# Norms at the start and between the blocks: root, squares and scaled tiles in PSUM, and the mean asked for elsewhere

## Chip, cores and metric

One core of a Trainium2 chip runs the kernel. The metric is the device time of one execution in microseconds (us), as the median of several runs. Before: 1818.57 us, median of 3 (1818.01 to 1822.48).

## What is computed

A transformer block pair on 512 tokens of width 1024, all in fp32. Block one: h = x + mixer(rms_norm(x)), then a gated ffn; block two the same with memory attention beside two others. Of this only the four norms named here and the small projections next to them matter:

```python
def rms_norm(x, g):
    y = x * rsqrt(mean(x * x, axis=-1) + eps)
    return y * g

u = rms_norm(x, norm_mix_g); z = u @ w_in                 # n_mix, the kernel's first work
h = h + (silu(g) * up) @ w_down                           # down1a, down1b: end of block one
x2 = rms_norm(h, norm_final_g)                            # n_fin
mkv = rms_norm(mem, g_mem) @ w_mem_kv                     # n_mem; mk and mv, 256 memory rows
u2 = rms_norm(x2, g_mix_pre_2); z2 = u2 @ w_in_2          # n_mix2
bias = rel_bias[rel_bucket(...)]                          # from buckets and relb, by two small matmuls
```

## The kernel before, in words

Activations lie transposed: 8 tiles (KT) of 128 rows by 512 tokens. A product in fp32 quality is made of three matmuls of the fp32r type, high by high, high by low and low by high (`split_mm`, lines 378 to 380); each side is split into a rounded high part and the rest.

The weights are one stream of 278 units of 128x1024. SyncE loads a unit into `w_raw` (three slots, R = 3), ScalarE copies it rounded into `w_hi` (`feed`, line 820), GpSimd subtracts to get `w_lo` (`low_part`, line 335), TensorE uses it. `feed_after(t)` makes unit t+2 and waits until unit t-1 has been used up. ScalarE, VectorE and GpSimd each work through one queue in program order, so a feed stands behind what was issued before it.

`tile_unit` is 24 matmuls into one bank, `token_unit` 12, `two_units` runs two units at once, tile k as soon as the norm's low part k is there. `down` runs eleven units over the ffn's hidden tiles into four banks. `acquire(b)` waits until the bank's last result was copied out.

A norm goes like this. ScalarE squares tile k (`square`), VectorE adds it to tmp[2] (`add_square`, line 1343), TensorE multiplies the sum by a matrix of ones to get the sum over rows (`norm`, line 514, bank 2), ScalarE makes the root with Ln and Exp into tmp[3] (`root`, lines 849 and 851). `norm_split` then runs on VectorE: scaled tile = hT x gain x root (line 1361), ScalarE copies it rounded to `u_hi` (line 864), VectorE subtracts to get `u_lo` (line 1355). Scaled tiles rotate through four buffers. For n_fin the product goes back into hT (line 1688) and the squares for n_mix2 follow it tile by tile.

The places: n_mix is the first thing the kernel does, its mean ahead of the first two units (gif and qkb 0), with the two bias matmuls behind these (lines 600, 601). n_mem's mean is asked for after down1a's first unit. n_fin's is asked for between mk 1 and mk 2, n_mix2's between mv 2 and mv 3; mk units use banks 4 and 5 in turn, mv units banks 6 and 7. ScalarE copies mk 0 and 1 out behind n_fin's root, mk 2 and 3 behind squares 3 and 5 of n_mix2, and feeds four units behind squares 0, 2, 4 and 6. In front of n_mix2's root it has the feeds behind mv 2 and mv 3's places in the stream, the last of which waits for the end of mv 2.

## Time and profile before

| what | us |
|---|---|
| median of 3 runs | 1818.57 |
| the profiled execution | 1820.88, its span 1819.1 |
| TensorE matmul busy | 1726.2, 95% of the span |
| VectorE busy | 869.7, 48% |
| GpSimd busy | 704.9, 39% |
| ScalarE busy | 625.1, 34% |

The span runs from the first instruction to the last. Busy time of TensorE is modelled at the ends of matmuls, so an idle stretch looks up to 0.2 us shorter than the time between two matmuls of a stream. In brackets behind a row stands the idle time before it and what ended it. The granted clock is the share of TensorE's full clock that the chip allows.

### The profile page before, as it was taken

The numbers are of one execution on the slowest core, as the hardware profiler recorded it, in microseconds if no ns is written. First come the engines' busy times: TensorE is split into PE (matmuls) and PEld (weight loads), VectorE is DVE, ScalarE is ACT, GpSimd is POOL, SyncE is SP. The second block draws the span as 40 slices with busy tenths as digits, with TensorE's granted clock in tenths as the row PEclk, the third lists the DMA queues.
The fourth block names the chain that finished last, engine by engine and source line by source line (L and its number), as shares of the span: only waits on it lengthen the run. The fifth ranks groups of instructions, "written<-read, shape, count | busy, mean of one in ns | idle before, by whom it ended". The sixth has DMA issues, their size and how long they took to land.

```text
span 1819.1 us, 23230 instructions
## 1 busy us (share of the span) xinstructions
PE 1726.2 (95%) x7880; PEld 1356.0 (75%) x7888; DVE 869.7 (48%) x1341; ACT 625.1 (34%) x997; POOL 704.9 (39%) x293
## 2 busy tenths in 40 slices
PE   5999999999999999998899899999999699999995
PEld 4888666777888887886578655668888488888884
DVE  6603665573655552035497756541332755555003
ACT  5233444434222223234424444453222422222221
POOL 2544222244544444444243111224444444444442
PEclk9999999999999999999999999999999899999998
DMA  4434311223322232234122111112332132232321
GB/s 154 160 130 117 103 58 47 69 72 115 113 94 92 94 103 93 93 104 151 61 93 74 43 36 35 59 45 95 94 102 93 36 115 92 92 103 94 103 93 46
DMA packets 46189, 162.21 MB, mean 89 GB/s; under 512 B 5564, under 2 KB 5692, under 8 KB 45864
## 3 DMA queue, kind: packets, MB, share of 16 engines
q1 hardware_dynamic: 42576, 151.16, 25.4%
q10 hardware_dynamic: 3544, 10.13, 1.7%
q8 instruction: 43, 0.70, 0.2%
q14 instruction: 26, 0.21, 0.0%
HBM read 156.91 MB, written 4.76 MB: 89 GB/s over the span
## 4 chain that ended last, share of the span: by engine, by line
PE 53%; issue 29%; POOL 10%; DVE 6%; ACT 2%; POOLq 0%; DVEq 0%; ACTq 0%
PE ps L378 16%; PE ps L380 16%; PE ps L379 16%; POOL w_lo L335 10%; PE ps L537 1%; PE ps L558 1%; DVE tmp L1343 1%; DVE tmp L1793 1%; PE ps L574 1%; PE ps L749 1%; DVE sum L1763 1%; PE ps L705 1%; DVE hT L1798 1%; PE ps L771 0%; PE ps L514 0%
## 5 line engine op out<-in xcount | busy, mean ns | idle before, releaser
L335 POOL TENSOR_TENSOR w_lo<-w_raw,w_hi 128x1024 fp32r<-128x1024 f32 x278 | 686.7, 2472 | 1068.4 <-ACT w_hi L820 1068.3
L378 PE MATMUL ps<-u_hi,w_hi 128*128 128x512 f32 x1392 | 565.1, 406 | 37.5 <-DVE u_lo L1355 11.6
L380 PE MATMUL ps<-u_hi,w_lo 128*128 128x512 f32 x1392 | 546.3, 392 | 0.0
L379 PE MATMUL ps<-u_lo,w_hi 128*128 128x512 f32 x1392 | 545.8, 392 | 0.0
L820 ACT ACTIVATE w_hi<-w_raw 128x1024 fp32r<-128x1024 f32 x278 | 292.7, 1055 | 425.5 <-PE ps L380 384.9
L378 PEld LDWEIGHTS ps<-u_hi,w_hi 128*128 128x128 f32 x1392 | 263.1, 189 | 117.0 <-issue 54.2
L380 PEld LDWEIGHTS ps<-u_hi,w_lo 128*128 128x128 f32 x1392 | 263.2, 189 | 56.4
L379 PEld LDWEIGHTS ps<-u_lo,w_hi 128*128 128x128 f32 x1392 | 263.6, 189 | 52.9 <-issue 2.4
L378 PE MATMUL ps<-a_hi,w_hi 128*128 (+1 forms) x352 | 137.2, 390 | 0.3 <-POOL w_lo L335 0.3
L380 PE MATMUL ps<-a_hi,w_lo 128*128 (+1 forms) x352 | 137.0, 389 | 0.0
L379 PE MATMUL ps<-a_lo,w_hi 128*128 (+1 forms) x352 | 137.0, 389 | 0.0
L1655 DVE TENSOR_TENSOR a_lo<-tmp,a_hi 128x512 f32 (+1 forms) x44 | 115.8, 2632 | 5.2
L1160 ACT ACTIVATE tmp<-tmp 128x512 f32<-128x512 f32 x44 | 27.8, 632 | 222.0 <-DVEq L1645 221.9
L1651 DVE TENSOR_TENSOR tmp<-ps,tmp 128x512 f32<-128x512 f32 x44 | 30.4, 692 | 100.5 <-PE ps L380 100.2
L378 PEld LDWEIGHTS ps<-a_hi,w_hi 128*128 128x128 f32 x352 | 66.1, 188 | 14.4 <-issue 0.8
L379 PEld LDWEIGHTS ps<-a_lo,w_hi 128*128 128x128 f32 x352 | 66.1, 188 | 13.8
L380 PEld LDWEIGHTS ps<-a_hi,w_lo 128*128 128x128 f32 x352 | 66.1, 188 | 13.7
L1643 DVE TENSOR_TENSOR tmp<-ps,tmp 128x512 f32<-128x512 f32 x44 | 30.4, 692 | 62.3 <-PE ps L380 49.5
L1809 DVE COPY o<-ps 128x512 f32<-128x512 f32 x8 | 5.5, 688 | 106.8 <-PE ps L380 106.8
L1613 DVE TENSOR_TENSOR tmp<-ps,tmp 128x512 f32<-128x512 f32 x16 | 11.1, 692 | 91.1 <-PE ps L380 90.0
L1679 DVE TENSOR_TENSOR hT<-ps,hT 128x512 f32<-128x512 f32 x8 | 5.5, 688 | 98.1 <-PE ps L380 98.1
L378 PE MATMUL ps<-m_hi,w_hi 128*128 128x512 f32 x128 | 50.0, 391 | 1.4 <-DVEq L1587 0.9
(279 smaller groups left out, 2160.7 us busy)
## 6 DMA issues: line engine op xcount, KB each, us to landing
w_raw<-stream SPq DMA_DIRECT2D x278, 512.0 KB, 3.5
g_rep<-g_one ACTq DMA_DIRECT2D x1, 2560.0 KB, 15.2
hT<-xT SPq DMA_DIRECT2D x4, 512.0 KB, 5.2
spread<-m_rows ACTq DMA_DIRECT2D x4, 512.0 KB, 4.6
tmp<-tmp ACTq DMA_DIRECT2D x32, 64.0 KB, 3.6
...
```

The costliest lines, as they stand in the source:

```text
L335: pool.tensor_tensor(w_lo[:, slot], w_raw[:, slot], w_hi[:, slot].bitcast(F32), ALU.subtract)\
L378: pe.matmul(out, wh, xh, start=start, stop=False)
L379: pe.matmul(out, wh, xl, start=False, stop=False)
L380: return pe.matmul(out, wl, xh, start=False, stop=stop)
L537: both.append(pe.matmul(ps[:, 2 + e, 0:keys[t]], head_q(h, t), head_k(h, keys[t]), start=True, stop=not extra(t)))
L558: m = pe.matmul(ps[p0:p1, b, t * P:t * P + P], values(h, kb), prT[e][:, kb * P:kb * P + P], start=kb == 0, stop=kb == nb - 1)
L574: m = pe.transpose(ps[:, 4 + e, kb * P:kb * P + P], pr[s % 4][:, kb * P:kb * P + P], ident)
L820: act.activation(w_hi[:, slot], w_raw[:, slot], ACT.Copy).then_inc(hi_ready, 1)
L1160: act.activation(tmp[0][:, :], tmp[1][:, :], ACT.Sigmoid).then_inc(named(name + "_e"), 1)
L1643: step(dve.tensor_tensor(tmp[1][:, :], ps[:, 0, :], tmp[3][:, :], ALU.mult))
L1651: step(dve.tensor_tensor(tmp[4][:, :], ps[:, 1, :], tmp[2][:, :], ALU.mult))
L1655: step(dve.tensor_tensor(a_lo[:, bass.ds(k, 1)], a, a_hi[:, bass.ds(k, 1)].bitcast(F32), ALU.subtract))
```

## The change

Buffers: n_mix, n_fin and n_mix2 keep the root in PSUM bank 3 (`norm_rs`); the scaled tiles of n_mix and n_mix2 take turns in banks 4 and 5, two deep in place of four; squares 1 to 7 of n_mix2 go to banks 0 and 1. n_mem keeps its SBUF tiles.

First norm: eight squares have buffers of their own; TensorE sums the first four by accumulating matmuls with a matrix of ones that VectorE sets, VectorE adds the last four and TensorE adds their sum. VectorE makes the first `w_lo`. Two weight units are loaded ahead of `kept`, and the bias inputs ahead of both; the bias matmuls stand ahead of the first two units, in banks 6 and 7.

Places: n_mem's mean and split come ahead of down1a's last unit, n_fin's mean in the middle of mk 1, n_mix2's in the middle of mv 2; mk units take banks 4 to 7. The three attentions share one set of semaphores with offsets in place of one set each (not shown; the same waits).

```diff
@@ buffers, counts
+        first_sq = ar("first_sq", [P, KT, T], F32, 24)
+        first_ones = ar("first_ones", [P, P], F32, 40)
...
+        OTHER_SUMS = {}
+        OTHER_SUMS["n_mix"] = {"sq": KT, "add": 3, "ms": 1, "rs": 1}
...
-        scaled = [tmp[4], tmp[5], tmp[0], tmp[1]]
+        norm_rs = ps[:, 3, :]
+        def scaled(name, k):
+            return [tmp[4], tmp[5], tmp[0], tmp[1]][k % 4][:, 0:MEM] if name == "n_mem" else ps[:, 4 + k % 2, :]
+        def square_at(name, k):
+            return ps[:, k % 2, :] if name == "n_mix2" and k > 0 else tmp[2 if k == 0 else k % 2][:, :]
@@ sync
             sp.dma_start(vec[:], vecs).then_inc(loads["vec"], 16)
+            sp.dma_start(buckets[:], tabs[0:32, TAB["buckets"]:TAB["buckets"] + 640]).then_inc(loads["bias_in"], 16)
+            sp.dma_start(relb_in[:], relb).then_inc(loads["bias_in"], 16)
+            for t in range(AHEAD):
+                sp.dma_start(w_raw[:, t], stream[t]).then_inc(landed[t], 16)
             sp.dma_start(kept[:], tabs[:, 0:KEPT]).then_inc(loads["kept"], 16)
-            for t in range(R):
+            for t in range(AHEAD, R):
                 sp.dma_start(w_raw[:, t], stream[t]).then_inc(landed[t], 16)
...
-            sp.dma_start(buckets[:], tabs[0:32, TAB["buckets"]:TAB["buckets"] + 640]).then_inc(loads["bias_in"], 16)
-            sp.dma_start(relb_in[:], relb).then_inc(loads["bias_in"], 16)
@@ gpsimd
-            ring(0, FIRST["ffn2"] + AHEAD)
+            pool.wait_ge(lo_ready, 1)
+            ring(1, FIRST["ffn2"] + AHEAD)
@@ tensor
-            def tile_unit(t, slot, b, xh, xl, n=T):
+            def tile_unit(t, slot, b, xh, xl, n=T, midway=None):
...
                 for k in range(KT):
+                    if midway and k == KT // 2:
+                        midway()
...
-            def token_unit(t, j, banks, xh, xl):
+            def token_unit(t, j, banks, xh, xl, midway=None):
...
                 for k2 in range(2):
+                    if midway and k2 == 1:
+                        midway()
@@ down
                 unit(u, u % R, *sides(0), first=True)
-                if after_first:
-                    after_first()
                 with pe.Fori(0, 3) as i:
...
+                if ahead_of_last:
+                    ahead_of_last()
                 if made:
                     pe.wait_ge(made, FT)
                 unit(u + 10, (u + 10) % R, *sides(20), last=True)
@@ tensor, the program's start
+            pe.wait_ge(named("set"), 2)
+            acquire(2)
+            for k in range(4):
+                pe.wait_ge(*of_norm("n_mix", "sq", k + 1))
+                pe.matmul(ps[:, 2, :], first_ones[:, :], first_sq[:, k], start=k == 0, stop=False)
+            pe.wait_ge(*of_norm("n_mix", "add", 3))
+            pe.matmul(ps[:, 2, :], first_ones[:, :], first_sq[:, 4], start=False, stop=True).then_inc(named("norm_ms"), 1)
+            pe.wait_ge(loads["bias_in"], 32)
+            acquire(6)
+            acquire(7)
+            pe.matmul(ps[0:NHA, 6, 0:320], relb_in[:, :], buckets[:, 0:320], start=True, stop=True)
+            pe.matmul(ps[0:NHA, 7, 0:320], relb_in[:, :], buckets[:, 320:640], start=True, stop=True)\
+              .then_inc(named("g_ps"), 1)
+            two_units(FIRST["gif"], u_hi, u_lo, T, ("n_mix", "lo"))
             pe.wait_ge(loads["kept"], 16)
-            norm("n_mix", T)
-            two_units(FIRST["gif"], u_hi, u_lo, T, ("n_mix", "lo"))
-
-            pe.wait_ge(loads["bias_in"], 32)
-            acquire(4)
-            acquire(5)
-            pe.matmul(ps[0:NHA, 4, 0:320], relb_in[:, :], buckets[:, 0:320], start=True, stop=True)
-            pe.matmul(ps[0:NHA, 5, 0:320], relb_in[:, :], buckets[:, 320:640], start=True, stop=True)\
-              .then_inc(named("g_ps"), 1)
@@ tensor, memory units
             for j in range(4):
                 t = FIRST["mk"] + j
-                if j == 2:
-                    norm("n_fin", T)
                 if j == 0:
                     pe.wait_ge(*of_norm("n_mem", "lo", KT))
-                tile_unit(t, t % R, 4 + j % 2, um_hi, um_lo, MEM)
+                tile_unit(t, t % R, 4 + j, um_hi, um_lo, MEM, (lambda: norm("n_fin", T)) if j == 1 else None)
             for j in range(4):
-                if j == 3:
-                    norm("n_mix2", T)
-                token_unit(FIRST["mv"] + j, j, [6, 7], um_hi, um_lo)
+                token_unit(FIRST["mv"] + j, j, [6, 7], um_hi, um_lo, (lambda: norm("n_mix2", T)) if j == 2 else None)
@@ scalar
-                    act.activation(tmp[k % 2][:, 0:n], src(k), ACT.Square).then_inc(named("norm_sq"), 1)
+                    act.activation(square_at(name, k)[:, 0:n], src(k), ACT.Square).then_inc(named("norm_sq"), 1)
...
-            def root(name, n, b=2):
+            def root(name, n, b=2, dst=None):
...
-                act.activation(tmp[3][:, 0:n], tmp[3][:, 0:n], ACT.Exp, scale=-0.5).then_inc(named("norm_rs"), 1)
+                act.activation(tmp[3][:, 0:n] if dst is None else dst, tmp[3][:, 0:n], ACT.Exp, scale=-0.5)\
+                   .then_inc(named("norm_rs"), 1)
...
-                square("n_mix", lambda k: hT[:, k], T, k)
+                act.activation(first_sq[:, k], hT[:, k], ACT.Square).then_inc(named("norm_sq"), 1)
...
-            root("n_mix", T)
+            root("n_mix", T, dst=norm_rs)
...
-                own.step(act.activation(mk[:, j, :], ps[:, 4 + j % 2, 0:MEM], ACT.Copy))
-                act.sem_inc(bank_free[4 + j % 2], 1)
+                own.step(act.activation(mk[:, j, :], ps[:, 4 + j, 0:MEM], ACT.Copy))
+                act.sem_inc(bank_free[4 + j], 1)
@@ scalar, down_act
                 feed_after(u)
-                if after_first:
-                    after_first()
...
+                    if ahead_of_last:
+                        ahead_of_last()
                     feed_after(u + 10)
@@ vector
-                dve.tensor_tensor(tmp[2][:, 0:n], tmp[2][:, 0:n], tmp[k % 2][:, 0:n], ALU.add)\
+                dve.tensor_tensor(tmp[2][:, 0:n], square_at(name, k)[:, 0:n], tmp[2][:, 0:n], ALU.add)\
...
+                depth, rs = (4, tmp[3][:, 0:n]) if name == "n_mem" else (2, norm_rs)
                 for k in range(KT):
-                    if k >= 4:
-                        dve.wait_ge(*of_norm(name, "lo", k - 3))
-                    dve.scalar_tensor_tensor(out=scaled[k % 4][:, 0:n], in0=src(k), scalar=v(gain, k),
-                                             in1=tmp[3][:, 0:n], op0=ALU.mult, op1=ALU.mult)\
+                    if k >= depth:
+                        dve.wait_ge(*of_norm(name, "lo", k - depth + 1))
+                    dve.scalar_tensor_tensor(out=scaled(name, k), in0=src(k), scalar=v(gain, k),
+                                             in1=rs, op0=ALU.mult, op1=ALU.mult)\
...
-            for k in range(KT):
-                add_square("n_mix", T, k)
+            step(dve.memset(first_ones[:, :], 1.0))
+            dve.sem_inc(named("set"), 1)
+            for k in range(5, KT):
+                dve.wait_ge(*of_norm("n_mix", "sq", k + 1))
+                if k > 5:
+                    dve.wait_ge(*of_norm("n_mix", "add", k - 5))
+                dve.tensor_tensor(first_sq[:, 4], first_sq[:, 4], first_sq[:, k], ALU.add).then_inc(named("norm_add"), 1)
+            dve.wait_ge(hi_ready, 1)
+            dve.tensor_tensor(w_lo[:, 0], w_raw[:, 0], w_hi[:, 0].bitcast(F32), ALU.subtract).then_inc(lo_ready, 1)
```

## Rows read from the trace of the kernel before

**Rows 1.** The page's busy shares: engine, busy us (share), instructions.

```profile
PE 1726.2 (95%) x7880; PEld 1356.0 (75%) x7888; DVE 869.7 (48%) x1341; ACT 625.1 (34%) x997; POOL 704.9 (39%) x293
```

**Rows 2.** The timeline, TensorE, first 36 us: start, us, engine, line, operation.

```profile
11.76 2.04 PE L514 MATMUL ps<-tmp,kept 128*128 128x512 f32 x2 [11.76 <-DVE tmp L1343]
21.11 0.77 PE L378 MATMUL ps<-u_hi,w_hi 128*128 128x512 f32 x1 [7.30 <-DVE u_lo L1355]
...
25.95 0.43 PE L380 MATMUL ps<-u_hi,w_lo 128*128 128x512 f32 x1
...
34.17 0.39 PE L380 MATMUL ps<-u_hi,w_lo 128*128 128x512 f32 x1
...
35.66 0.50 PE L378 MATMUL ps<-u_hi,w_hi 128*128 128x512 f32 x1
```

**Rows 3.** The timeline, TensorE and ScalarE around the memory norm.

```profile
686.01 0.67 PE L514 MATMUL ps<-tmp,kept 128*128 128x256 f32 x2 [1.64 <-DVE tmp L1343]
...
694.28 1.99 ACT L820 ACTIVATE w_hi<-w_raw 128x1024 fp32r<-128x1024 f32 x2
```

**Rows 4.** The timeline, TensorE, 801 to 841 us.

```profile
801.45 0.28 PE L378 MATMUL ps<-um_hi,w_hi 128*128 128x256 f32 x1
...
807.21 1.02 PE L514 MATMUL ps<-tmp,kept 128*128 128x512 f32 x2
810.16 0.36 PE L378 MATMUL ps<-um_hi,w_hi 128*128 128x256 f32 x1 [1.93 <-ACTq L1201]
...
829.71 1.10 PE L514 MATMUL ps<-tmp,kept 128*128 128x512 f32 x2 [2.27 <-DVE tmp L1343]
...
836.22 0.47 PE L378 MATMUL ps<-u_hi,w_hi 128*128 128x512 f32 x1 [2.67 <-DVE u_lo L1355]
...
840.79 0.50 PE L378 MATMUL ps<-u_hi,w_hi 128*128 128x512 f32 x1 [1.61 <-DVE u_lo L1355]
```

**Rows 5.** The timeline, VectorE and GpSimd, first 22 us.

```profile
6.15 5.47 DVE L1343 TENSOR_TENSOR tmp<-tmp,tmp 128x512 f32<-128x512 f32 x7 [5.28 <-ACT tmp L845]
...
12.42 7.40 POOL L335 TENSOR_TENSOR w_lo<-w_raw,w_hi 128x1024 fp32r<-128x1024 f32 x3 [11.97 <-ACT w_hi L820]
...
15.40 4.97 DVE L1361 SCALAR_TENSOR_TENSOR tmp<-hT,vec,tmp 128x512 f32<-128x512 f32 x2 [3.78 <-ACT tmp L851]
...
20.29 0.68 DVE L1355 TENSOR_TENSOR u_lo<-tmp,u_hi 128x512 fp32r<-128x512 f32 x1
```

**Rows 6.** The timeline, VectorE, final norm and n_mix2.

```profile
809.73 3.03 DVE L1688 SCALAR_TENSOR_TENSOR hT<-hT,vec,tmp 128x512 f32<-128x512 f32 x3 [3.74 <-ACT tmp L851]
...
832.32 3.03 DVE L1361 SCALAR_TENSOR_TENSOR tmp<-hT,vec,tmp 128x512 f32<-128x512 f32 x2 [2.75 <-ACT tmp L851]
```

**Rows 7.** Three lines of VectorE: operation, operands, count: min/median/max ns, starts.

```profile
L1655 DVE TENSOR_TENSOR a_lo<-tmp,a_hi x44: 691/2676/2772, 455.1 to 1679.4; 128x512 f32 x42, 128x512 fp32r<-128x512 f32 x2
...
L1643 DVE TENSOR_TENSOR tmp<-ps,tmp x44: 691/692/692, 449.3 to 1672.6; 128x512 f32<-128x512 f32 x44
...
L1459 DVE SCALAR_TENSOR_TENSOR tmp<-ps,vec,tmp x24: 746/749/751, 38.6 to 77.6; 128x511 f32<-128x511 f32 x8, 128x510 f32<-128x510 f32 x8, 128x509 f32<-128x509 f32 x8
```

**Rows 8.** The timeline, ScalarE, first 36 us.

```profile
4.67 0.63 ACT L840 ACTIVATE tmp<-hT 128x512 f32<-128x512 f32 x1 [2.64 <-DMA hT<-xT]
...
11.28 1.06 ACT L820 ACTIVATE w_hi<-w_raw 128x1024 fp32r<-128x1024 f32 x1 [0.59 <-DMA w_raw<-stream]
12.56 1.06 ACT L820 ACTIVATE w_hi<-w_raw 128x1024 fp32r<-128x1024 f32 x1 [0.22 <-DMA w_raw<-stream]
13.85 0.69 ACT L849 ACTIVATE tmp<-ps,small 128x512 f32<-128x512 f32 x1 [0.23 <-PE ps L514]
...
35.77 0.43 ACT L975 ACTIVATE gvals<-ps 8x320 f32<-8x320 f32 x1 [0.64 <-PE ps L601]
```

**Rows 9.** The timeline, ScalarE, in front of n_mix2's root.

```profile
826.96 2.15 ACT L820 ACTIVATE w_hi<-w_raw 128x1024 fp32r<-128x1024 f32 x2
```

**Rows 10.** A stretch: engines' busy us, PEclk, DMA share, GB/s.

```profile
811.00:812.00 1.00, 1.00 (x7) 1.00 (x7) 0.93 (x2) 0.63 (x1) 0.00 (x0) 0.54 0.71 209
```

82 lines of the change are left out of this document (42 added, 40 removed).

## Prediction

> **What bounds the kernel now.** I read the page's busy shares first: the matmul engine works for 95% of the span [rows 1]. In the long loops nothing is to be had unless a matmul goes away, so the value of this change lies in the places where TensorE stands still around a norm. I looked for these in TensorE's order of time and found four: the start, until 21.11 us [rows 2]; the mean of the memory norm, 1.64 us of waiting at 686 us [rows 3]; the final norm's mean with the k projection of the memory after it, 1.93 us before 810.16; and the second block's first norm, three waits from 827 to 841 us [rows 4]. Then I read VectorE, GpSimd and ScalarE beside each place, because the wait's name tells only who came last.
>
> The reader should see one thing there above all. VectorE's scaled product (the nearest undisturbed form, at line 1459, takes 0.75 us) took 4.97 us for two while GpSimd was in its three subtractions (12.42 to 19.82) [rows 5]; at 809.73 three took 3.03, and the two at 832.32 took 3.03 [rows 6]. All read two SBUF tensors. The same happens 42 times to the ffn's subtraction (median 2.68, fastest 0.69), while the ffn's product with a PSUM operand took 0.691 to 0.692 in all 44 and the convolution's three-operand form with one PSUM operand 0.746 to 0.751 in all 24 [rows 7]. So an instruction of VectorE with two SBUF inputs waits until GpSimd's instruction is over, and one with a PSUM input does not. The change gives the products (root in bank 3), the low parts (scaled tile in banks 4, 5) and the squares' sums of n_mix2 a PSUM input.
>
> **First norm.** Now: squares from 4.67, last sum at 11.62, mean by TensorE 11.76 to 13.80, ScalarE's Ln at 13.85, the first product at 15.40, first low part 20.29 to 20.97, TensorE at 21.11 [rows 2, 5, 8].
>
> Weights: the first two feeds (11.28, 12.56) wait for their DMA, 1.28 us for 512 KB, or 0.40 MB/us [rows 8]. `kept` (384 KB) now goes behind the first two tiles and `buckets` (80 KB) ahead: 304 KB less, 0.76 us. Feed 1 then ends at 12.56 + 1.06 - 0.76 = 12.86.
> The sum: TensorE takes five fp32 matmuls in place of one. The one cost 2.04 us; four pitches of the slow matmuls at 21 us (0.427 each) are 1.71. TensorE starts at about 5.4 and doubled its pace 4.84 us after it began at 21.11 [rows 2]; if it does so here, three go at 1.71 (to 10.5), the fourth to about 11.5, and the fifth, whose sum VectorE has by 11.62 even if nothing there is sooner, to 12.7. If it stays slow, the fifth ends between 14.0 and 15.6. I take 12.7. Then Ln is bound by feed 1: 12.95, that is 0.9 sooner, and the first product begins at 14.5.
> VectorE now also makes the first w_lo: from 512 columns in 0.69 (the fastest of the 44) about 1.2 us for 1024, in 11.6 to 12.8, when it would idle. GpSimd starts its two at 12.9 and 15.4; TensorE needs only the first, at 15.3.
> Products at 14.5 and 15.2 without GpSimd's lock. ScalarE's third feed (after Exp, 1.06) ends at 15.35 and holds the first high part to 15.4 to 16.05; low part 16.1 to 16.8; TensorE at 16.9. The two units thus begin 4.2 us sooner. From there I let TensorE be slow for 4.84 us as now, so the end also moves by 4.2. At the fast pace 36 matmuls took from 25.95 to 34.17, 0.228 each, so a tile of the two units takes 1.36 and a unit 5.44. If TensorE keeps that pace across the idle 3 us, VectorE sets the end: two instructions plus the wait that depth 2 adds, 0.68 + 0.75 = 1.43 per tile, 16.8 + 7 x 1.43 + 1.36 = 28.2 against 34.40 now: 6.2 us. The bounds are 2.2 (five slow matmuls) and 6.2.
> The two bias matmuls leave the place behind the units, where 34.40 to 35.66 is not the units' work. But behind the gate unit ScalarE's queue (rows, bias values, their DMA, then feed 3 and GpSimd's 2.40) was as late as TensorE, so only its own 0.64 us of waiting for those matmuls [rows 8] comes out: 0.65 (0 to 1.26). Subtotal 4.9.
>
> **Memory norm.** The mean is asked for ahead of the eleventh unit of down1a. The first unit's wait goes: 1.64 in the trace, 1.8 from the true end of the matmul before. So does most of the gap it left at 697.9 (feeds two and three stood behind the split on ScalarE until 694.28 [rows 3]), 0.5. The matmul itself, 0.5, only moves. What is queued behind it in its new place: ScalarE's feed for the unit two further on, 694.28 - 686.01 = 8.3 us after the mean is asked for, 0.7 less as GpSimd idles then; 1.06 and 2.40 later w_lo is there, at 11.2, and TensorE comes at 0.5 + 2 x 5.44 = 11.4. Next VectorE's four sums into hT and ScalarE's four squares of n_fin now start after the split and hold the following feed until about 13.2; w_lo at 16.7, wanted at 16.8. Both just fit, with 0.1 to 0.2 us to spare. Gain 2.3; if the chain is a microsecond longer, 1.0.
>
> **Final norm and n_mix2.** Two units of 256 columns take 807.21 - 801.45, 2.88 each [rows 4]. The mean is now asked for at 805.77 but the eighth square's sum ends at 806.00: TensorE waits 0.4, the mean goes at 806.15, 1.06 sooner than 807.21, and the product x0 starts at 808.7 against 809.73. It is not locked, nor are the other seven and the sums. Then ScalarE carries the stretch: eight squares of 0.63 [rows 8], four feeds (two took 1.99 [rows 3]), two copies of mk, in one queue. I walked it: squares at 809.65, 811.4, 812.0, 813.55, 814.75, 816.2, 817.25; copies of mk 2 and 3 at 814.1 and 816.75. The units mk 2 and 3 have banks of their own (6, 7) and no longer wait (1.93 now). But mv 0 needs these banks: it waits for the second copy from 815.3 to 817.2, a new wait of 1.9 us. It ends at 819.3, feed mv 3 (which waits for it) at 820.4, square seven 821.0, sum 821.7. The mean of n_mix2, in the middle of mv 2, is asked for at 823.4 without a wait (now 829.71, after 2.27). Its result, 824.5, doesn't help at once: ScalarE has the feed that waits for the end of mv 2 (825.7) ahead of the root, as it has now [rows 9], so Ln comes at 826.95 instead of 830.85. First product 828.4, low part 830.55, TensorE 830.65 instead of 836.22: 5.6 us. ScalarE's feed and copies of mv between high parts 1 and 2 remain (2.5 us), so the 1.8 us stop at tile 2 shrinks to 1.0; after it VectorE's 1.43 a tile stands against TensorE's 1.36. End at 842.8 instead of 849.0 to 849.1 (840.79 and six tiles): 6.3.
> The stretch from 811.07 to 814.5 ran at the lower level, granted 0.54 in its first microsecond [rows 10], after TensorE had stood from 808 to 810; it is in the trace's times and not in my walk. If such a fall comes in the mv units instead (after the new wait), it takes up to 1.7. Bounds 4.5 and 6.8.
> No instruction here shows VectorE reading and writing PSUM at once, nor ScalarE writing 512 columns there. The lower bound is a little less than their SBUF times (0.1 us), the upper 0.2 us more (Ln, which reads PSUM, takes 0.69 against 0.63). I take SBUF's; 0.1 more on each adds about 2 us over both norms.
> The Trainium skill, "VectorE: DVE Perf Modes", section "The TRN2 errata", gives a PSUM source 120 cycles of fixed cost where an SBUF source has 58. That speaks against the change by an estimated 0.065 us an instruction, or 1.1 us over tiles 0 to 7 of n_mix2, 1806.2 for the forecast. The rows show none of it: 0.692 with PSUM, 0.691 at best without [rows 7], and the measurement decides.
> Joining the attention semaphores, exchanging the operands of the sum, and the order of the later loads move nothing: the counts and waits are the same instructions, and the loads are wanted only after 28 us.
>
> **Sum.** 4.9 + 2.3 + 6.3 = 13.5 us of the traced span, 1819.1 to 1805.6 (that execution took 1820.88, 2.3 above the median of 1818.57). Taken off the median: 1805.1.
>
> **Rivals.**
> A, the early sum stays slow or the clock falls again: the first norm gives 2.2 + 0.65, and a fall among the mv units takes 1.7. For it: TensorE idled for 3 us before the first units, and the fall at 811. Against: the quick rise at 25.95. 1805.1 + 2.0 + 1.7 = 1808.8.
> B, the moved waits of the memory norm and mv 0 bite harder: the two margins of 0.1 to 0.2 us are smaller than what I can read, and every late feed repeats on TensorE. 1.3 lost there and 1 to 2 us at mv 0: 1808.
> C, the change doesn't do what it says: GpSimd blocks these instructions whatever the operand. Then the first norm gives about 1.9 + 0.65 and the other two 2.3 and 1.1: 6 us, 1812.6. The 68 undisturbed instructions with a PSUM input speak against it.
> D, slower: reading and writing PSUM in one VectorE instruction costs twice the time, 1.5 us, because every tile also crosses ScalarE's reads and TensorE's writes there. A tile then takes 2.84: first norm 16.8 + 0.7 + 7 x 2.84 + 1.36 = 38.7 against 34.4, n_mix2 852.5 against 849.1, eight products and seven sums of the final norm some 5 more, less 2.9 kept elsewhere: 1828. It decides from about 1.3 us an instruction, where 13.5 us are used up. Nothing in the rows is near it.
> E, TensorE keeps its fast pace from its early matmuls: 2.0 more, 1803.
>
> **How the numbers follow.** Forecast 0.48, A 0.14, B 0.17, E 0.12, C 0.06, D 0.03. The range takes in E and A with the 0.1 us an instruction that I could not price, 1801.0 to 1811.0 (each end 2 us beyond E and A), and leaves out C, D and the tails. A measurement tells about 0.3%, 5.5 us, from no change, so faster means under 1813.1: forecast, A, B, E and most of C, 0.94; the same 0.03; slower 0.03.
>
> **What would show it.** Right: no product or low part of n_mix, n_mix2 and no product of the final norm above 0.8 us beside GpSimd; TensorE's first units near 16.9 and its third unit near 36; no wait of TensorE at 684 and none above 0.3 near 745; a wait of about 1.9 us in the first mv unit; Ln of n_mix2 right behind a feed. Wrong: the first Ln later than 13.9 (sum slow), these instructions at 1.5 to 3 us (C, D), a wait for GpSimd at the first or second unit of down1b (B), or the lower clock among the mv units (A).

## Result and profile after

The changed kernel takes 1808.33 us in the median of 7 executions (1805.75 to 1812.89), the kernel before 1818.17 of 7 (1817.62 to 1822.48). The ratio is 0.9944, 95% interval [0.9933, 0.9956]: 10.2 us less (9.8 between the medians). That is inside the predicted range and 3.2 above the forecast of 1805.1. The profiled execution of the new kernel was its fastest, 1805.75, with a span of 1804.0 us; that of before took 1820.88, span 1819.1. So the two profiles lie 15.1 us apart, 5 more than the kernels do, and they can't be subtracted end to end. They can be compared stage by stage. The busy share of the page:

```profile
PE 1726.7 (96%) x7896; PEld 1354.7 (75%) x7896; DVE 855.5 (47%) x1339; ACT 623.5 (35%) x997; POOL 701.5 (39%) x292
```

TensorE's work is what it was, and its share of the shorter span has gone from 95 to 96% [rows 1].

TensorE's first 60 us, in the profile after (start, duration, engine, line, operation, tiles, and in brackets how long it stood idle before and who ended that):

```profile
5.60 5.70 PE L621 MATMUL ps<-first_sq,first_ones 128*128 128x512 f32 x8 [5.60 <-ACT first_sq L980]
...
11.38 1.12 PE L623 MATMUL ps<-first_sq,first_ones 128*128 128x512 f32 x2
...
16.99 0.76 PE L398 MATMUL ps<-u_hi,w_hi 128*128 128x512 f32 x1 [3.32 <-DVE u_lo L1380]
...
19.68 0.52 PE L398 MATMUL ps<-u_hi,w_hi 128*128 128x512 f32 x1
...
30.27 0.47 PE L398 MATMUL ps<-u_hi,w_hi 128*128 128x512 f32 x1 [0.75 <-ACTq L996]
...
55.59 0.47 PE L398 MATMUL ps<-u_hi,w_hi 128*128 128x512 f32 x1 [2.50 <-DVEq L1495]
```

Before, one matmul of 2.04 us at 11.76 made the mean and the first unit began at 21.11 [rows 2]. Now four squares and VectorE's partial sum go through TensorE from 5.60 on, and the first unit begins at 16.99. Further down a wait of 0.75 us for ScalarE is new, at 30.27, and one of 2.50 us for VectorE stands at 55.59.

VectorE and GpSimd in the same stretch:

```profile
14.73 1.41 DVE L1387 SCALAR_TENSOR_TENSOR ps<-hT,vec,ps 128x512 f32<-128x512 f32 x2 [1.44 <-ACT ps L875]
16.15 0.69 DVE L1380 TENSOR_TENSOR u_lo<-ps,u_hi 128x512 fp32r<-128x512 f32 x1
...
41.09 2.43 POOL L354 TENSOR_TENSOR w_lo<-w_raw,w_hi 128x1024 fp32r<-128x1024 f32 x1 [0.94 <-ACT w_hi L844]
...
41.29 2.77 DVE L1512 TENSOR_TENSOR rows<-rows 4x512 f32<-4x512 f32 x1
...
49.54 2.70 DVE L1515 TENSOR_TENSOR rows<-rows 4x512 f32<-4x512 f32 x1
```

The two products at 14.73 took 1.41 together, where the two at 15.40 had taken 4.97 [rows 5]. But the row subtraction at line 1512, two SBUF operands of 4 rows, takes 2.77. Here are the same subtraction and its neighbour in the profile of before, and TensorE's one wait behind them:

```profile
46.35 0.68 DVE L1479 TENSOR_TENSOR rows<-rows 4x512 f32<-4x512 f32 x1
...
46.40 2.90 POOL L335 TENSOR_TENSOR w_lo<-w_raw,w_hi 128x1024 fp32r<-128x1024 f32 x1 [1.19 <-ACT w_hi L820]
...
58.56 0.47 PE L378 MATMUL ps<-u_hi,w_hi 128*128 128x512 f32 x1 [0.82 <-DVEq L1462]
```

There VectorE started 0.05 us ahead of GpSimd, took 0.68, and it was GpSimd's instruction that was longer (2.90 for 2.43). In the kernel after GpSimd started 0.20 us ahead and VectorE waited; TensorE's wait behind it has grown from 0.82 to 2.50 us.

The memory norm: no wait of TensorE at 684 us any more (1.64 before, [rows 3]) and none above 0.1 us near 745.

Between the blocks (TensorE, ScalarE, VectorE):

```profile
801.14 1.10 PE L538 MATMUL ps<-tmp,kept 128*128 128x512 f32 x2 [0.21 <-DVE tmp L1368]
...
812.24 0.50 PE L398 MATMUL ps<-w_hi,um_hi 128*128 128x512 f32 x1 [1.69 <-ACTq L1226]
...
818.49 1.02 PE L538 MATMUL ps<-tmp,kept 128*128 128x512 f32 x2
...
825.65 0.47 PE L398 MATMUL ps<-u_hi,w_hi 128*128 128x512 f32 x1 [2.01 <-DVE u_lo L1380]
...
821.00 1.06 ACT L844 ACTIVATE w_hi<-w_raw 128x1024 fp32r<-128x1024 f32 x1 [2.55 <-PE ps L400]
821.97 0.67 ACT L873 ACTIVATE tmp<-ps,small 128x512 f32<-128x512 f32 x1
...
823.39 1.41 DVE L1387 SCALAR_TENSOR_TENSOR ps<-hT,vec,ps 128x512 f32<-128x512 f32 x2 [6.45 <-ACT ps L875]
```

The waits of 2.27 for the mean of n_mix2, 2.67 for its first low part and 1.61 at a later one [rows 4] have become none, 2.01 and 0.57. The wait of 1.93 at 810.16, in which the third memory key unit stood for a bank, is gone; one of 1.69 at 812.24, for a bank that ScalarE's copy of a later key frees, stands in the first memory value unit instead.

VectorE's instructions in this stretch, grouped by form (count, then busy time and mean ns of one), first the two products in the kernel before, then the kernel after:

```profile
L1688 DVE SCALAR_TENSOR_TENSOR hT<-hT,vec,tmp 128x512 f32<-128x512 f32 x8 | 10.9, 1374 | 3.8 <-ACT tmp L851 3.7
L1361 DVE SCALAR_TENSOR_TENSOR tmp<-hT,vec,tmp 128x512 f32<-128x512 f32 x8 | 9.6, 1212 | 2.8 <-ACT tmp L851 2.8
```

```profile
L1387 DVE SCALAR_TENSOR_TENSOR ps<-hT,vec,ps 128x512 f32<-128x512 f32 x8 | 5.9, 755 | 6.7 <-ACT ps L875 6.4
L1721 DVE SCALAR_TENSOR_TENSOR hT<-hT,vec,ps 128x512 f32<-128x512 f32 x8 | 5.8, 741 | 3.1 <-ACT ps L875 2.7 <-ACTq L865 0.3
L1380 DVE TENSOR_TENSOR u_lo<-ps,u_hi 128x512 fp32r<-128x512 f32 x8 | 5.5, 686 | 0.9 <-ACT u_hi L889 0.8
```

None of the products is lengthened by GpSimd any more: the 16 took 0.74 to 0.76 us each. The eight low parts took 0.68 to 0.69; they had not been lengthened here before either (mean 0.683).

To see where the gain arises and where it goes, I use ScalarE's feeds, the 278 copies of a weight unit into w_hi: the n-th in one profile against the n-th in the other. "Lead" is by how much the new kernel is ahead at that feed. It contains up to 0.6 us (-0.9 in bias_back) by which the first feed came at another time than in before, because its weights landed then. The words behind the unit numbers are the kernel's names for its groups of units. The runs in the right columns are described below.

| feed of unit (counted from 0) | before, us | lead of after | start_alone | rest_alone | in_sbuf | row_psum | start_row | all_four |
|---|---|---|---|---|---|---|---|---|
| 3, convolution | 37.52 | 5.5 | 4.5 | 0.1 | 1.9 | 5.0 | 3.8 | 5.7 |
| 7, convolution | 59.08 | 3.0 | 2.0 | 0.1 | -0.7 | 6.6 | 5.4 | 7.3 |
| 26, ka | 160.13 | 2.8 | 0.6 | 0.1 | -0.7 | 5.7 | 4.4 | 6.4 |
| 80, ffn | 533.50 | 2.8 | 0.6 | -1.9 | -0.5 | 5.7 | 2.8 | 6.4 |
| 120, down1b | 752.69 | 5.3 | 0.7 | 0.6 | 2.0 | 8.3 | 2.8 | 8.9 |
| 138, iq | 849.47 | 11.5 | 0.6 | 5.5 | -1.8 | 12.9 | 2.8 | 18.3 |
| 160, aq | 995.08 | 12.4 | 0.6 | 6.8 | -1.9 | 14.1 | 2.5 | 19.4 |

In the column of after: 5.5 ahead after the start, 3.0 four units later, 5.3 behind the memory norm (+2.5), 11.5 behind the norms between the blocks (+6.2). The lead at the start is given back by half within 25 us. The rest of the way to 15.1 arises in code that is the same in both. It fits the clock: TensorE runs at the lower of its two clock levels (granted 0.5, 1.2 of 2.4 GHz) in stretches of 3.4 to 13.7 us and at the very end, and these stretches are not equally long in the two executions (6.8 us at 869 in before, 3.4 at 860 in after; 13.7 at 1419 against 10.2 at 1406). I call the start of such a stretch a fall of the clock.

The gain between the blocks differs among kernels that have the same code there. Between the feeds of units 120 and 138 the lead grows by 6.2 us in after and in warm, but by 4.6 in row_psum, 4.5 in bias_back, 4.8 in sum_by_vector and 4.9 in rest_alone. In these four the clock falls right behind the new wait of 1.7 to 1.9 us, and in the other two it does not. Windows behind that wait in bias_back (wait until 812.97) and in warm (until 814.41), with stretch, length, busy time and count of TensorE, of weight loads, VectorE, ScalarE and GpSimd, then the granted clock, DMA share and GB/s:

```profile
814.00:816.00 2.00, 2.00 (x6) 1.63 (x5) 0.84 (x2) 0.00 (x0) 0.53 (x1) 0.50 0.86 256
```

```profile
816.00:818.00 2.00, 2.00 (x11) 1.65 (x10) 0.28 (x1) 1.17 (x2) 0.03 (x1) 1.00 0.60 178
```

So a fall there costs 1.3 to 1.7 us, and the one profile of after, its fastest execution, is one without it.

### The profile page after: what moved, and what is told of

Its sections match the earlier page's. It is cut to its first block, busy times and chain, and to the rows that moved or that the text cites. A ratio compares the mean times of both kernels' runs of the same rounds, so it can differ in the third digit from the quotient of the medians.

```text
span 1804.0 us, 23102 instructions
## 1 busy us (share of the span) xinstructions
PE 1726.7 (96%) x7896; PEld 1354.7 (75%) x7896; DVE 855.5 (47%) x1339; ACT 623.5 (35%) x997; POOL 701.5 (39%) x292
## 4 chain that ended last, share of the span: by engine, by line
PE 85%; DVE 9%; ACT 2%; issue 2%; DMA 1%; SPq 0%; ACTq 0%; DVEq 0%; POOLq 0%; POOL 0%
PE ps L398 26%; PE ps L400 25%; PE ps L399 25%; PE ps L561 2%; PE ps L582 2%; PE ps L598 1%; DVE tmp L1826 1%; DVE tmp L1368 1%; PE ps L773 1%; DVE sum L1796 1%; PE ps L567 1%; PE ps L677 1%; DVE hT L1831 1%; DVE tmp L1492 1%; PE ps L729 1%
## 5 line engine op out<-in xcount | busy, mean ns | idle before, releaser
L398 PE MATMUL ps<-u_hi,w_hi 128*128 128x512 f32 x1392 | 564.2, 405 | 34.2 <-DVE u_lo L1398 11.9
L398 PE MATMUL ps<-w_hi,u_hi 128*128 128x512 f32 x128 | 50.4, 394 | 0.8 <-ACTq L909 0.8
```

Source lines behind the costliest of these rows:

```text
L398: pe.matmul(out, wh, xh, start=start, stop=False)
```

## Experiments

All times are medians; the ratio is to the kernel before, run beside them on the same chip. Its medians there were 1818.41 (start_alone, rest_alone, in_sbuf, row_psum), 1818.88 (mk_back, root_first, bias_back, all_four), 1818.58 (sum_by_vector, warm, four_banks) and 1819.66 (start_row). Line numbers in their profiles differ a little from those of after.

**start_alone** and **rest_alone**: the change in two halves. Edit of the first, in the kernel after, shortened (the other half is the mirror image, with the start's lines of TensorE, ScalarE, VectorE and SyncE and GpSimd's first low part put back):

```diff
-            return ps[:, k % 2, :] if name == "n_mix2" and k > 0 else tmp[2 if k == 0 else k % 2][:, :]
+            return tmp[2 if k == 0 else k % 2][:, :]
...
-            root("n_mix2", T, dst=norm_rs)
+            root("n_mix2", T)
...
-                tile_unit(t, t % R, 4 + j, um_hi, um_lo, MEM, (lambda: norm("n_fin", T)) if j == 1 else None)
+                if j == 2:
+                    norm("n_fin", T)
+                tile_unit(t, t % R, 4 + j % 2, um_hi, um_lo, MEM)
...
-                if ahead_of_last:
-                    ahead_of_last()
```

> The kernel after, with the memory norm, the final norm and the norm behind it put back as they were before (asked between units, root, squares and scaled tiles in SBUF, memory keys in banks 4 and 5): only the first norm's part of the change is left. Theory (the start gains 5.1 us at the third unit and the locked row subtraction beside GpSimd gives 2.3 of it back): VectorE's row subtraction takes 2.77 us again, TensorE waits about 2.5 us near 55.6 us, the feed of unit 6 and all that follow run 2.8 us ahead of before, and the time is about 1815.4 us, 2.8 under before. Rival (the gain is carried through, the give-back in the one profile was chance): 5.1 us ahead at unit 6 and later, about 1813.1 us.

Measured: 1820.17 us of 12, ratio 1.0005 [0.9994, 1.0016]. Neither the theory's 1815.4 nor the rival's 1813.1: alone, the start's part gains nothing in the median. The column of the table says where it goes: 4.5 ahead, 2.0 at unit 7 and 0.6 from the next stage on. The first step is the locked subtraction. The second is seen in TensorE's first matmul behind the wait and in the windows (stretch, length, busy time and count of TensorE, of weight loads, VectorE, ScalarE, GpSimd, then the granted clock of TensorE, DMA share and GB/s):

```profile
56.58 0.77 PE L398 MATMUL ps<-u_hi,w_hi 128*128 128x512 f32 x1 [2.44 <-DVEq L1499]
```

```profile
56.00:58.00 2.00, 1.42 (x4) 1.17 (x4) 1.60 (x3) 1.43 (x2) 0.00 (x0) 0.52 0.00 0
58.00:60.00 2.00, 2.00 (x7) 1.63 (x6) 1.93 (x3) 0.15 (x1) 1.78 (x1) 0.62 0.00 0
```

After it had waited 2.44 us TensorE ran at half its clock for about 3 us and lost 1.4 us of lead. The profiled execution of the kernel after has the same wait at 55.59 and kept its clock (1.00 in the three windows of 2 us from 54 to 60). The 12 executions fall in two groups, five between 1813.9 and 1816.6 and seven between 1820.1 and 1822.4, which fits falls that come in some and not in others. The fall at 56 us alone can't be the difference: the groups' medians, 1816.1 and 1820.9, are 4.9 us apart, and it cost 1.4. What else differs is not shown.

> The kernel after, with the first norm's part put back as before (VectorE's seven additions, GpSimd's first low part, root and scaled tiles in SBUF, loads and bias matmuls in their old places): only the memory norm and the norms between the blocks are changed. Theory: nothing differs up to 680 us, 2.3 us gained at the memory norm, 6.2 between the blocks, 8.5 in sum: about 1809.7 us; together with the start alone that is 11.3, so 1.2 more than the whole change measured (10.1), which then is spread of the clock. Rival (the parts help one another: the steps between the blocks gain less or more without the start): anything under 7 or over 10 us.

Measured: 1811.37 us of 6, ratio 0.9966 [0.9954, 0.9978], 6.2 to 7.0 us. In the profile the lead goes from -1.9 at the ffn to 0.6 behind the memory norm (2.5) and to 5.5 at iq (4.9, with the fall of the clock behind the new wait): 7.4 for both, where the theory had 8.5. The 1.3 more at aq arise in code that is the same, behind a fall that is shorter here (3.4 us at 865) than in before (6.8 at 869). It had lost 1.8 us before, near 194 us, in a fall of the clock (0.70 and 0.50 in the windows from 192 to 196) that the profile of before does not have. The sum of the halves, +0.9 and -6.2 by the ratios, is far from the -10.2 of the whole. Falls of the clock are part of each half's time and would not add; that they are the whole difference is not shown.

**in_sbuf**: the orders of the change without the way round the port.

```diff
-            return [tmp[4], tmp[5], tmp[0], tmp[1]][k % 4][:, 0:MEM] if name == "n_mem" else ps[:, 4 + k % 2, :]
+            return [tmp[4], tmp[5], tmp[0], tmp[1]][k % 4][:, 0:MEM if name == "n_mem" else T] if name in ('n_mem', 'n_mix', 'n_mix2') else ps[:, 4 + k % 2, :]
...
-            root("n_mix", T, dst=norm_rs)
+            root("n_mix", T)
...
```

> The kernel after, with all orders as they are but root, squares and scaled tiles of the first norm, the final norm and the norm behind it in SBUF again (scaled tiles four deep): the early asking and TensorE's part of the sum without the way round the port. Theory (lock and asking each carry a share): VectorE's products beside GpSimd take 2.7 to 5 us a pair again, the third unit starts 2 to 3 us later than in the kernel after but ends up where it was by unit 6, since that gain is given back there anyway; between the blocks about 2 us are lost; time about 1810.8 us, 2.5 over the kernel after (1808.3). Rival A (the lock was the whole of the gain): 6 us or more over it, above 1814. Rival B (the lock was off the path): no difference, 1808.3.

Measured: 1822.65 us of 11, ratio 1.0022 [1.0013, 1.0031]: 14.3 us over the kernel after, and slower than before. That is rival A, and twice what it asked for. The theory's give-back at the start failed too: the lead at unit 7 is -0.7, 3.6 us behind that of after. The rows:

```profile
14.76 4.37 DVE L1387 SCALAR_TENSOR_TENSOR tmp<-hT,vec,tmp 128x512 f32<-128x512 f32 x2 [1.43 <-ACT tmp L875]
...
814.45 2.82 DVE L1721 SCALAR_TENSOR_TENSOR hT<-hT,vec,tmp 128x512 f32<-128x512 f32 x1
...
818.39 0.77 PE L398 MATMUL ps<-w_hi,um_hi 128*128 128x512 f32 x1 [5.61 <-ACTq L1226]
```

The products of the stretch from 797 to 850 us, grouped by form (count, busy time, mean ns):

```profile
L1721 DVE SCALAR_TENSOR_TENSOR hT<-hT,vec,tmp 128x512 f32<-128x512 f32 x8 | 11.9, 1492 | 2.8 <-ACT tmp L875 2.8
L1387 DVE SCALAR_TENSOR_TENSOR tmp<-hT,vec,tmp 128x512 f32<-128x512 f32 x8 | 8.9, 1122 | 5.4 <-ACT tmp L875 5.4
```

Eight products of the final norm took 11.9 us instead of 5.8 (10.9 in before). ScalarE's copy of the third memory key stands behind squares that wait for these products, and TensorE waits 5.61 us for its bank. Between the blocks the lead falls by 3.7 us (2.0 to -1.8) where the kernel after gains 6.2. Part of that is the clock, which stands at its lower level from 816.3 to 826.5 in this execution, so for 8 us behind that wait. So with these banks the early asking has no gain of its own there: it moves VectorE's products onto GpSimd's instructions and behind a bank that is freed late, and pays only where PSUM operands keep the products short. The memory norm, in SBUF in all these kernels, keeps its 2.5 (-0.5 to 2.0).

**row_psum**: the row that both long subtractions read is put in PSUM.

```diff
+row2 = ps[0:4, 4, :]
-step(dve.tensor_tensor(rows[:, 1, :], rows[:, 1, :], rows[:, 2, :], ALU.subtract))
+step(dve.tensor_tensor(rows[:, 1, :], rows[:, 1, :], row2, ALU.subtract))
...
```

> The kernel after, with one row of the gates (the row that both long subtractions read) kept in PSUM bank 4 instead of SBUF, so that these subtractions have only one operand in SBUF. Theory (they wait for GpSimd as long as both operands lie in SBUF, and this is what gives back the start's gain): the two subtractions take 0.7 us each instead of 2.77 and 2.70, TensorE's waits of 0.18 and 2.50 us near 47 and 55 us go, the feed of unit 6 is 5.1 to 5.5 us ahead of the kernel before instead of 2.8, and the time is about 1805.7 us, 2.6 under the kernel after (1808.3). Rival (the give-back has another cause, such as VectorE's convolution being the bound by itself or GpSimd's low parts late): subtractions short, but TensorE waits as before and the time stays at 1808.3.

Measured: 1805.09 us of 5, ratio 0.9927 [0.9912, 0.9941], 3.2 us below the kernel after. The two intervals overlap a little ([0.9933, 0.9956] there), so I read the lead as well.

```profile
41.79 0.68 DVE L1513 TENSOR_TENSOR rows<-rows,ps 4x512 f32<-4x512 f32 x1
...
47.95 0.67 DVE L1516 TENSOR_TENSOR rows<-rows,ps 4x512 f32<-4x512 f32 x1
...
41.59 2.44 POOL L355 TENSOR_TENSOR w_lo<-w_raw,w_hi 128x1024 fp32r<-128x1024 f32 x1 [0.94 <-ACT w_hi L845]
...
30.76 0.47 PE L399 MATMUL ps<-u_hi,w_hi 128*128 128x512 f32 x1 [0.75 <-ACTq L997]
```

The subtraction starts 0.20 us behind GpSimd's instruction, as in the kernel after, and takes 0.68. The wait at 30.76 is TensorE's last before 75 us. The lead is 6.6 at unit 7 and settles at 5.7 from unit 11 on, where after has 3.0: 2.7 us, near the theory's 2.6. Its intermediate figure, 5.1 to 5.5 at the feed of unit 6, fails: it was 4.6. The mechanism holds: with one operand moved the long subtractions and the wait behind them are gone.

**start_row**: start_alone with the row in PSUM.

> The kernel of the run start_alone (only the first norm's part of the change), with the gates' row in PSUM bank 4 as in row_psum. Start_alone took the time of before although its third unit starts 4.5 us sooner. Theory (that gain was lost to the two locked subtractions, 2.3 us, and to half pace of TensorE from 56.6 to 59 us behind the wait they cause, some 1.5 us more): subtractions of 0.7 us, no wait of TensorE near 56 us, no stretch at the lower clock there, the feeds from 60 us to 680 us 5.2 to 5.9 us ahead of before, and the time 1812.4 to 1813.5 us. Rival (the loss of start_alone lay elsewhere, in a clock that falls in the later stages by another amount): feeds at 700 us less than 4 us ahead or a time of 1815 us and over.

Measured: 1815.45 us of 9 (four of them between 1812.2 and 1813.1), ratio 0.9974 [0.9963, 0.9986], against 1.0005 without the edit: 5.6 us for an edit whose two subtractions take 4.1 us less. No wait and no fall near 56 us; the lead is 5.4 at unit 7 and 4.5 at unit 15, where start_alone had 0.6. But the median is above the theory's 1812.4 to 1813.5, and what the rival asked for came true: 1815 us or over, and a lead under 4 at 700 us (2.8). The profiled execution was the slowest of the nine and shows one reason: a fall of the clock further on, where a short stretch of attention leaves TensorE partly idle:

```profile
186.00:188.00 2.00, 0.66 (x1) 0.50 (x2) 1.66 (x4) 1.50 (x3) 1.16 (x1) 0.81 0.74 229
188.00:190.00 2.00, 2.00 (x3) 0.68 (x2) 1.72 (x3) 0.90 (x3) 1.19 (x1) 0.50 0.17 66
```

It costs 1.6 us (lead 4.4 to 2.8). This pair settles the loss of the first 100 us. The rival is right about the rest: more is lost in the later stages, and where and in how many executions the clock falls there is open.

**bias_back**: the two bias matmuls behind the first two units again.

```diff
-            pe.matmul(ps[0:NHA, 6, 0:320], relb_in[:, :], buckets[:, 0:320], start=True, stop=True)
...
             two_units(FIRST["gif"], u_hi, u_lo, T, ("n_mix", "lo"))
+            pe.matmul(ps[0:NHA, 6, 0:320], relb_in[:, :], buckets[:, 0:320], start=True, stop=True)
...
```

> The kernel after, with the two bias matmuls behind the first two units again, as before (their new banks 6 and 7 kept). The prediction put their move at 0.65 us of gain and did not name a wait behind them. Theory (the wait of 0.75 us for bank 0, which ScalarE's copies of the gate rows free, lies where they lay): the two matmuls of about 0.6 us each cover that wait, the third unit ends at most 0.5 us later than in the kernel after, and the copies of the bias values on ScalarE wait longer; 1808.3 to 1808.8 us. Rival (the move was worth its 0.65 us and more): 1809.0 us or over.

Measured: 1807.83 us of 5, ratio 0.9935 [0.9921, 0.9948]: not slower than the kernel after, and by half a us faster, which the intervals can't tell from nothing. That lies below both the theory and the rival. At the feed of unit 3 the feeds are 0.66 us later against their own start, so up to there the move brings what the prediction said. But then:

```profile
42.70 0.68 DVE L1512 TENSOR_TENSOR rows<-rows 4x512 f32<-4x512 f32 x1
...
42.75 2.90 POOL L354 TENSOR_TENSOR w_lo<-w_raw,w_hi 128x1024 fp32r<-128x1024 f32 x1 [1.20 <-ACT w_hi L844]
...
54.90 0.47 PE L398 MATMUL ps<-u_hi,w_hi 128*128 128x512 f32 x1 [0.83 <-DVEq L1495]
```

VectorE is 0.05 us ahead of GpSimd once more, takes 0.68 as in the kernel before, and TensorE waits 0.83 us instead of 2.50. The moved matmuls turned the order round. From unit 6 on the lead is 3.7, against 3.0 in after, although this execution's first feed came 1.2 us later (12.17 against 10.98): counted from the first feed, having the bias matmuls ahead cost 1.9 us by then in this pair of profiles, where it was to bring 0.65. A fall of the clock at 189 us, which after does not have, takes 1.6 of that lead again.

**mk_back**: the memory keys in banks 4 and 5 again (`4 + j` becomes `4 + j % 2`).

> The kernel after, with the memory keys of units 2 and 3 in banks 4 and 5 again instead of 6 and 7 (ScalarE's copies too). Theory (since the early asking, ScalarE's copy of memory key 3 stands behind squares, and the first memory value unit waits 1.69 us for its bank): that wait goes; the third key unit now waits up to 0.9 us for the copy of the first (it ends at 804.0, TensorE is free at about 803.2); net the first mv unit starts 0.8 to 1.1 us earlier and the kernel takes about 1807.3 us. Rival (the last addition of the next norm, behind a feed and a square, sets the end here): mv starts earlier but the two indexer units do not, 1808.3 us.

Measured: 1809.49 us of 5, ratio 0.9945 [0.9932, 0.9959], no difference that can be told. In the profile the wait of 1.69 is gone, one of 0.51 stands at 804.51, and between the feeds of units 120 and 138 the lead grows by 7.2 us (4.97 to 12.16) where it grew by 6.2 in after (5.32 to 11.48). That is 1.0 more, as the theory says, in a profile each; the median is no better than that of after.

**root_first**: the root of n_mix2 ahead of ScalarE's last feed.

```diff
-for j in (2, 3):
-    feed_after(FIRST["mv"] + j)
-root("n_mix2", T, dst=norm_rs)
+feed_after(FIRST["mv"] + 2)
+root("n_mix2", T, dst=norm_rs)
+feed_after(FIRST["mv"] + 3)
```

> The kernel after, with the root of the norm between the blocks ahead of ScalarE's last feed there instead of behind it. Theory (the feed waits 2.55 us for TensorE's mv unit, with the mean square ready at 819.6 and the logarithm run at 821.97): the logarithm starts 2.3 us earlier, VectorE's first product at about 821.0 instead of 823.39, TensorE's wait of 2.01 us ahead of the indexer's units shrinks to about 0 to 0.2, and the kernel takes about 1806.3 us. Rival (the moved feed is then late for its unit or the first pairs wait for the copies of the memory values): the gain is given back within two units, 1808.3 us.

Measured: 1810.31 us of 5, ratio 0.9946 [0.9931, 0.9960]. TensorE's wait of 2.01 is replaced:

```profile
826.45 0.51 PE L398 MATMUL ps<-u_hi,w_hi 128*128 128x512 f32 x1 [0.96 <-POOL w_lo L354]
```

0.96 us for GpSimd's low part of the second indexer unit. The lead grows by 7.8 us over the stretch (3.45 to 11.24) instead of 6.2: 1.6 of the 2.0 expected. The profiled execution, which is the median one, lost about as much earlier, in the fall at 56 to 59 us that start_alone has too (its lead is 0.8 at 160 us, not 2.8).

**all_four**: row_psum, mk_back and root_first together, the last square ahead of the feed in front of it, and the first convolution unit in bank 2.

```diff
-                if k in (0, 2, 4, 6):
+                if k in (0, 2, 4, 7):
                     feed_after(FIRST["mk"] + 2 + k // 2)
...
-                tile_unit(u + j, (u + j) % R, (j + 1) % 2, u_hi, u_lo)
+                tile_unit(u + j, (u + j) % R, 2 if j == 1 else (j + 1) % 2, u_hi, u_lo)
```

> The kernel after with five small edits: the gates' row in PSUM, the keys' banks 4 and 5, the root ahead of the last feed, the last square ahead of the feed in front of it, and the first convolution unit behind the gates in bank 2 instead of bank 0. Theory (each removes a wait of its own, 3.3 us measured for the row, 0.8 to 1.1, 2.0 and 0.75 for the others): about 1801.2 us, TensorE with no wait of over 0.5 us between 17 and 100 us and none of over 0.6 between 800 and 835. Rival (the later ones meet the same limit, GpSimd's low part of the first indexer units): the gain between the blocks stays at 1 us and the time at 1803.5 us.

Measured: 1800.94 us of 4, ratio 0.9905 [0.9888, 0.9922]: 17.3 us under the kernel before, 7.4 under the kernel after. Three of TensorE's waits from 14 to 840 us, in total, times, longest (those left out stand in the attention and ffn stages):

```profile
PE ps L399 <- DVE u_lo L1381: 3.4, 1, 3.4
...
PE ps L399 <- DVEq L1496: 1.2, 1, 1.2
PE ps L399 <- POOL w_lo L355: 1.0, 1, 1.0
```

Two expectations about waits fail. The wait for bank 0 becomes one of 1.15 us for bank 1 at 35.90, because VectorE's first convolution ends at 35.7 whatever bank the next unit has. And GpSimd's 1.0 stays ahead of the indexer. The gain between the blocks is 9.4 (8.9 to 18.3), so the rival's "1 us" fails too. It is 3.2 more than in after and 4.8 more than in row_psum: the wait of 1.7 us is gone here, and with it the fall of the clock that came behind it in row_psum.

**four_banks**: all_four with the convolution units rotating over four banks (`(j + 1) % 4`).

> The kernel of the run all_four, with the convolution units rotating over banks 0 to 3 instead of two of them (1, 2, 3, 0 and again). Theory (in all_four TensorE's second convolution unit waits 1.15 us for bank 1, since VectorE's first convolution ends only at 35.7 us; with four banks VectorE may be late by two units): no wait of TensorE between 17 and 75 us, feeds after it 1.1 us ahead of all_four, about 1799.9 us against 1800.9. Rival (feeds of ScalarE, which stand behind VectorE's convolution in its order, take the wait's place: GpSimd's low part comes late): a wait for GpSimd's w_lo of 0.5 to 1.2 us and the time of all_four.

Measured: 1800.52 us of 4, ratio 0.9896 [0.9880, 0.9911], which can't be told from all_four. The 1.15 is replaced by the rival's wait:

```profile
35.54 0.50 PE L399 MATMUL ps<-u_hi,w_hi 128*128 128x512 f32 x1 [0.65 <-POOL w_lo L355]
```

**sum_by_vector**: VectorE adds all squares of the first norm.

```diff
-            for k in range(5, KT):
+            for k in range(1, KT):
...
-                dve.tensor_tensor(first_sq[:, 4], first_sq[:, 4], first_sq[:, k], ALU.add)
+                dve.tensor_tensor(first_sq[:, 0], first_sq[:, 0], first_sq[:, k], ALU.add)
```

> The kernel after, with the first norm's sum made by VectorE alone (seven additions, one matmul for the mean, as before) and all else as it is. Theory (TensorE's four early squares bring two things: one matmul of 1.1 us instead of one of 2.04 at the end of the sum, and a faster pace of the first units): the logarithm runs 0.3 us later than 13.24, TensorE keeps half pace for 4.8 us from 17.3 us on instead of 2.7, the third unit begins 1.3 to 1.5 us later than in the kernel after; behind unit 6 what is left of it depends on whether the long subtraction starts ahead of GpSimd's instruction. Time 1808.3 to 1809.7 us. Rival (TensorE would have its fast pace at once if it had not worked early): third unit at the same time or up to 1 us sooner.

Measured: 1808.74 us of 5, ratio 0.9953 [0.9940, 0.9967]. The mean takes one matmul of 2.04 us at 11.78, TensorE's first unit starts at 17.63 (16.99), and the third unit (31.14 against 30.27) 0.9 us later, where 1.3 to 1.5 were expected. TensorE's share in the sum is thus worth 0.6 us at the first unit, of the 4.1 by which it moved. The half pace lasted 3.1 us (17.63 to 20.75), not 4.8.

**warm**: three matmuls that do nothing, in TensorE's idle time ahead of the first unit.

```diff
+for _ in range(3):
+    pe.matmul(ps[:, 1, :], first_ones[:, :], first_sq[:, 0], start=True, stop=True)
 two_units(FIRST["gif"], u_hi, u_lo, T, ("n_mix", "lo"))
```

> The kernel after, with three more fp32 matmuls of 512 columns into bank 1 between the bias matmuls and the first two units, in the 3.3 us in which TensorE stands idle; their result is overwritten. Theory (the half pace from 16.99 to 19.7 us comes from that idle time): the granted clock stays at its upper level, the two units run at VectorE's pace of 1.38 us a tile from the start and end 1.2 us sooner, at about 28.1 instead of 29.36 us; the third unit starts 1.2 us sooner. Behind it the two long subtractions and the convolution take most of it back: 1807.3 to 1808.3 us. Rival (the fall comes on its own, whatever TensorE does there): 16.99 to 19.7 as in the kernel after.

Measured: 1807.82 us of 5, ratio 0.9942 [0.9928, 0.9955]. The first units in this kernel, the windows there, and the same windows of the kernel after (last of the three listings):

```profile
17.22 0.47 PE L398 MATMUL ps<-u_hi,w_hi 128*128 128x512 f32 x1
17.52 0.39 PE L399 MATMUL ps<-u_lo,w_hi 128*128 128x512 f32 x1
```

```profile
16.00:18.00 2.00, 1.97 (x7) 0.87 (x6) 1.96 (x4) 1.05 (x3) 2.00 (x2) 1.00 0.63 178
18.00:20.00 2.00, 2.00 (x10) 1.59 (x9) 1.93 (x4) 1.10 (x2) 0.40 (x1) 1.00 0.79 252
```

```profile
16.00:18.00 2.00, 1.01 (x3) 0.85 (x4) 1.96 (x4) 1.05 (x3) 2.00 (x1) 0.63 0.64 195
18.00:20.00 2.00, 2.00 (x6) 1.61 (x5) 1.93 (x4) 0.86 (x2) 0.15 (x1) 0.52 0.73 223
```

Ten matmuls in 2 us instead of six. The third unit starts 1.2 us sooner, counted from the first feed. It is no gain at the end: 2.46 us of wait at 54.63, and this time a fall of the clock from 56 to 60 us and another near 190. Kept busy, TensorE did not fall at the start, so the rival, that it would fall whatever it does, is out for this place (in one execution).

## Why the prediction was right, and where not

The sign, the mechanism and two of the three terms hold; the time was 3.2 us over the forecast.

*The lock and the way round it* hold. Every product, low part and sum of squares that got a PSUM operand took 0.68 to 0.76 us, beside GpSimd too. Rival C (GpSimd blocks whatever the operand) and rival D (reading and writing PSUM costs twice) needed 1.5 to 3 us. in_sbuf and row_psum show both directions: operands put back, 14.3 us lost; two more taken out, 3.2 won. ScalarE's writes of 512 columns into PSUM, which no row had shown, took 0.60 us (L875), where 0.63 was assumed.

*Memory norm, 2.3*: measured 2.5 at unit 120. One of the two margins of 0.1 to 0.2 us was just missed: TensorE pauses 0.3 us at 747 us and the lead is 5.0 from unit 121 on, so 2.2 stay. Rival B is out there.

*Final norm and n_mix2, 6.3*: measured 6.2 where the clock does not fall, 4.5 to 4.9 where it does. The new wait of 1.9 measured 1.69, the logarithm does stand behind a feed. The prediction gave the gain to the mean asked for early and to the short products as one walk. in_sbuf shows that the first without the second, with the banks as they are, would have been a loss of 3.7, a lower clock included.

*First norm, 4.9*: it is there, even a little more: the unit behind the third begins at 36.10 instead of 41.24, 5.1 us sooner. The steps: the fifth matmul was to end at 12.7 and ended at 12.5, the logarithm at 12.95 and ran at 13.24, the first unit at 16.9 and came at 16.99. One step had its size wrong without harm: half pace from there for 4.84 us, while 2.7 were measured, which is the 0.9 us that the two units ended sooner than walked (29.36, not 30.2); the wait of 0.75 us at 30.27, which no step had, took most of that away. The prediction's own sign, "its third unit near 36", does not fit its walk: the third unit began at 35.66 in before and at 30.27 after; 36.10 is where it is over. Rival E did not come: the clock was up from 9.7 us on and fell at 16.5, in the idle time; warm shows what it would have brought, 1.2 us at the third unit.

**The step that failed is in the sum: the first norm's 4.9 us are carried from the third unit to the end of the span**, and no work is named that the moved start meets. Of them 3.0 were left at unit 7. The prediction had the rule in its own second paragraph, two SBUF inputs wait until GpSimd is over, and its bias step ("only its own 0.64 us of waiting for those matmuls ... comes out: 0.65") ended at the third unit. The next instructions of VectorE with two SBUF inputs beside GpSimd stand 9 and 11 us further on: the first product behind the convolution (1.20 us at 39.49, 0.95 in before) and the subtraction at line 1479 of before (1512 after). The subtraction ran free in the trace of before by a start of 0.05 us. In after it takes 2.1 us more. With it TensorE's wait in front of a later convolution unit grew from 0.82 to 2.50 us and one of 0.18 us came up at 47.41, and its lead went from 5.1 us (36.10 against 41.24) to 3.0 (55.59 against 58.56). row_psum and the pair start_alone and start_row show that these are cause and effect.

With 3.0 in place of 4.9 the sum is 11.6, or 1807.0; measured 1808.3. Of what is left, two things are seen, and neither is counted out. TensorE falls to its lower level behind the wait at 56 us in start_alone, root_first and warm (1.4 to 1.8 us of lead lost) and not behind the same wait in after, mk_back, sum_by_vector and in_sbuf. And it falls behind the new wait between the blocks in four profiles of seven, for 1.3 to 1.7 us. The second is what rival A named, "the lower clock among the mv units", at 1.7; with 4.7 in place of 6.3 the sum would be 10.0, near the measured 10.2, but the only profile of after does not have this fall, so the match may be luck. Rival A's other half, the slow sum, did not come (Ln at 13.24, not after 13.9). That the time lies near its 1808.8 is no evidence for the whole of it.

What stays open: how often the clock falls at 56, at 190 and at 812 us, and how much of the spread of after (1805.75 to 1812.89) it makes. Each kernel has one profile only. With effects of 1 to 2 us from single edits, medians of 4 to 12 executions hardly decide; the lead of the feeds does, up to the next fall.
